# Biased attention heads: a band of near distances and four residue classes in place of the full square

## The reference

```python
DIL_PATTERNS = ((128, 1), (512, 4), (2048, 16))

def dilated_window_attention(q, k, v, rel_bias, window, dilation):
    w = window // (2 * dilation)
    ...
    mask = (np.abs(rel) <= w)[None] & ((key_l >= 0) & (key_l < L))[:, None, :]
    bias = jnp.transpose(rel_bias[t5_bucket(rel * dilation)], (2, 0, 1))
    logits = jnp.einsum('brnqhd,brnkhd->brnhqk', qs, kw) * (dh ** -0.5) + bias
    ...
    e = jnp.exp(logits - m)
    den = jnp.sum(e, axis=-1, keepdims=True)
    o = jnp.einsum('brnhqk,brnkhd->brnqhd', (e / den), vw)
```

## Time and profile before

| | us |
|---|---|
| median of 3 runs | 3556.62 (3554.47 to 3556.8) |
| profiled execution | 3552.48 |
| its span | 3550.7 |
| PE busy | 3451.8 (97%) |
| DVE busy | 2068.9 (58%) |
| ACT busy | 1715.8 (48%) |
| POOL busy | 1659.0 (47%) |

### The profile page before, as it was taken

One profiled execution on the slowest core, in us unless ns is written; L12 is line 12 of the kernel. 1 busy time (PEld: TensorE's weight loads), 2 busy tenths in 40 slices (PEclk: granted clock), 3 DMA queues, 4 the chain that ended last, 5 costly groups with the idle time before them and its releaser, 6 DMA issues. The chain is left out here.

```text
span 3550.7 us, 47741 instructions
## 1 busy us (share of the span) xinstructions
PE 3451.8 (97%) x17305; PEld 2858.6 (81%) x17305; DVE 2068.9 (58%) x3148; ACT 1715.8 (48%) x2973; POOL 1659.0 (47%) x1239
## 2 busy tenths in 40 slices
PE   8999999999899999999999999999998999999998
PEld 7788777778788888888777887777787888888886
DVE  4234888964745555455651358799366455554555
ACT  4343888974444434411353358789553344343113
POOL 1133554443477676423342435534345776763223
PEclk9999999999999999999999999999999999999999
DMA  5442320122122121422324413211232121213213
GB/s 181 128 104 75 77 75 23 42 84 96 53 68 78 58 78 58 144 80 82 118 70 135 127 52 90 57 34 32 75 107 67 62 78 59 78 58 137 95 66 119
DMA packets 247439, 292.81 MB, mean 82 GB/s; under 512 B 43244, under 2 KB 197182, under 8 KB 247167
## 3 DMA queue, kind: packets, MB, share of 16 engines
q1 hardware_dynamic: 247207, 289.76, 27.0%
HBM read 202.70 MB, written 80.31 MB: 80 GB/s over the span
## 5 line engine op out<-in xcount | busy, mean ns | idle before, releaser
L1709 DVE TENSOR_TENSOR pl<-ps,ph 128x512 fp32r<-128x512 f32 (+1 forms) x576 | 376.4, 654 | 66.4 <-ACT ps L1540 65.9
L1432 PE MATMUL ps<-q,k 97*128 97x512 f32 (+4 forms) x1296 | 387.1, 390 | 17.2 <-DVE pl L1709 7.0
L3098 DVE TENSOR_TENSOR y<-ps,y 128x512 f32<-128x512 f32 (+1 forms) x432 | 260.2, 602 | 230.8 <-PE ps L291 227.7
L1539 ACT ACTIVATE ph<-ps 128x512 fp32r<-128x512 f32 (+1 forms) x576 | 329.2, 572 | 135.2 <-PE ps L1432 130.6
L1540 ACT ACTIVATE ps<-ps 128x512 f32<-128x512 f32 (+1 forms) x576 | 328.4, 570 | 0.0
L1432 PEld LDWEIGHTS ps<-q,k 97*128 97x128 f32 (+2 forms) x1296 | 234.4, 189 | 86.3 <-DVE pl L1709 24.5
L1670 DVE TENSOR_REDUCE mx<-ps 128x1 f32<-128x512 f32 x352 | 242.0, 688 | 40.6 <-PE ps L1461 32.5
L1444 PE MATMUL ps<-ph,vh 128*128 128x512 f32 (+1 forms) x576 | 227.4, 395 | 0.0
L1445 PE MATMUL ps<-ph,vl 128*66 128x512 f32 (+1 forms) x576 | 219.7, 381 | 0.0
L1447 PE MATMUL ps<-pl,vh 128*128 128x512 f32 (+1 forms) x576 | 219.7, 381 | 0.0
L289 PE MATMUL ps<-hh,wh 128*128 128x512 f32 (+1 forms) x528 | 200.5, 380 | 10.1 <-PEq L283 6.2
(11 more groups left out here) (396 smaller groups left out, 10193.9 us busy)
## 6 DMA issues: line engine op xcount, KB each, us to landing
activations<-c_gate SPq DMA_DIRECT2D x44, 640.0 KB, 3.8
act_in<-activations SPq DMA_DIRECT2D x20, 1280.0 KB, 5.7
raw<-in_w_up SPq DMA_DIRECT2D x48, 512.0 KB, 4.9
up_raw<-in_w_up SPq DMA_DIRECT2D x40, 512.0 KB, 4.7
raw<-in_w_down SPq DMA_DIRECT2D x40, 512.0 KB, 3.5
heads<-stage SPq DMA_DIRECT2D x28, 640.0 KB, 3.5
rq<-heads SPq DMA_DIRECT2D x56, 320.0 KB, 4.0
raw<-in_w_in SPq DMA_DIRECT2D x32, 512.0 KB, 4.4
```

The costliest lines, as they stand in the source:

```text
L1432: mm = pe.matmul(out, a, b, start=(k == 0), stop=(k == len(prods) - 1))
L1539: act.activation(c.ph[g % RING][:, 0:w], scores, ACT.Exp, scale=STEP_SCALE[kind(h)]).then_inc(exp_done, 1)
L1709: dve.tensor_tensor(c.pl[g % RING][:, 0:w], bank(c, ST + g % 3, w), c.ph[g % RING][:, 0:w].bitcast(F32), ALU.subtract).then_inc(p_low, 1)
L3098: dve.tensor_tensor(y, bank(c, down_bank(it, u), w), y, ALU.add).then_inc(down_added, 1)
```

## The change

A biased head has ten steps in place of 18: two for the short sequence as before, four for the residue classes and four for the near band. In a class step all 256 keys of one residue modulo 4 meet the 256 queries of that residue, in two tiles of 128 keys; the table holds there only the distances above 64. In a near step two tiles of 128 keys meet the queries within 64 tokens of them, as four runs, one for each residue. Together they cover each unmasked pair once.

The q operand of the long sequence is stored by residue (`by_class`). The values are loaded a second time, by residue (`vh_class`, `vl_class`), and split by DVE. The tables `th` and `tl` are 1024 wide and come from new lines in memory (`distance_parts`). For the maxima of biased heads an fp32 table (`dense`) is loaded; PE fills two banks with 1024 scores of a tile of queries (`side_scores`) and DVE compares them in one instruction (`take_side`). The rest of the side work is placed by a table `side_at`.

```diff
-    STEPS = []
+    def class_step(r):
+        tiles, values = [], []
+        for u, half in enumerate((1, 0)):
+            tiles.append((slice(512 * half + r, 512 * half + 512, 4), 256 * r, CLASSES + P * u, 256 * u, 256, 0))
+            for q in range(2):
+                values.append(("class", 4 * half + r, 2 * q, P * r, 256 * u + P * q, P, 0, u == 0 and r == 0))
+        return tiles, values, {0: [0], 2: [2]}.get(r, []), []
+    def near_step(kts, ends):
+        for kt in kts:
+            qa, qb = max(0, kt * P - REACH), min(1024, kt * P + P + REACH)
...
+    SPLIT_STEPS += [class_step(r) for r in range(4)]
+    SPLIT_STEPS += [near_step((0, 7), []), near_step((1, 2), []), near_step((3, 4), [0]), near_step((5, 6), [2])]
...
+        elif kind(h) == "B":
+            for u, i in enumerate((2, 3, 4, 5, 6, 6, 7, 8, 9)):
+                put(h - 1, i, "side", h, u)
+            put(h - 1, 7, "row", h, 0)
+            put(h - 1, 8, "row", h, 1)
+            put(h, 0, "row", h, 2)
...
+                def side_scores(h, u):
+                    for n in range(2):
...
+                        mm = pe.matmul(bank(c, SIDE + n, w), c.q1[h % 3][:, q * P:q * P + P], c.k1[kv(h)][:, keys][:, ::-1], start=True, stop=True)
...
+                        region = c.ps[:, (SIDE + n) * 512:(SIDE + n) * 512 + w]
+                        dve.tensor_tensor_reduce(out=region, in0=region, in1=c.dense[h % 2][:, x0:x0 + w], scale=-1.0, scalar=3.0e38,
+                                                 op0=ALU.add, op1=ALU.min, accum_out=c.m[:, m0:m0 + 1]).then_inc(max_taken, 1)
...
+                def split_class_values(h):
+                    dve.tensor_copy(hi, raw).then_inc(class_hi, 1)
...
+                load_q(2)
+                for h in range(HEADS - 2):
+                    if kind(h) == "B":
+                        move_row(h, 2)
+                    if kind(h + 1) == "B":
+                        load_parts(h + 1)
+                    if kind(h + 2) == "B" and kind(h) == "B":
+                        load_dense(h + 2)
...
+                        for r in range(2):
+                            move_row(h + 1, r)
+                        load_q(h + 3)
...
+                sp.dma_start(c.s_parts, c.d_masked).then_inc(line_stored, 16)
+                sp.wait_ge(line_stored, 32)
...
+                    sp.dma_start(c.s_parts[:, CLASS_LINE + n0:CLASS_LINE + n1],
+                                 c.s_line[:, 3 + 4 * n0:3 + 4 * n1:4], allow_slow_non_contiguous=True).then_inc(line_stored, 16)
```

More of the change, by code:

```diff
@@ L1272, in row_tiles, with steps, place, step_width @@
         return ROW_TILES[r][1] - ROW_TILES[r][0]
+    def steps(h):
+        return SPLIT_STEPS if kind(h) == "B" else PLAIN_STEPS
+    FROM = [0]
+    for h in range(HEADS):
+        FROM.append(FROM[-1] + len(steps(h)))
+    G_TOTAL = FROM[HEADS]
+    G_END = G_TOTAL + PV_LAG + 4
+    PLACE = [(h, i) for h in range(HEADS) for i in range(len(steps(h)))]
+    def place(g):
+        return PLACE[g] if g < G_TOTAL else (HEADS, g - G_TOTAL)
+    def step_width(h, i):
+        return sum(tile[4] for tile in steps(h)[i][0])
@@ L1274, in third_row @@
+    OUTPUTS = [(h, block, g) for g, (h, i) in enumerate(PLACE) for block in steps(h)[i][3]]
+    OUTPUT = {(h, block): o for o, (h, block, _) in enumerate(OUTPUTS)}
     def third_row(h):
         return 19 - max_lead(h)
-    def side_work(h, i):
[L1280 to L1289, removed]
@@ new lines, in free_blocks @@
+    def free_blocks(h, i):
+        return [0, 2] if kind(h) == "B" and i == 2 else [] if kind(h) == "B" and i > 2 else steps(h)[i][2]
+    def side_work(h, i):
+        work = side_at.get((h, i), [])
+        return sorted(work, key=lambda item: (item[0] == "row", item[1], item[2]))
+    side_order = [item for g in range(G_TOTAL) for item in side_work(*place(g))]
+    side_banks, taken_after, turn = {}, {}, 0
+    TAKEN, READY = [0, NM], [0, 2]
+    for h in range(1, HEADS):
+        TAKEN.append(TAKEN[h] + (10 if kind(h) == "B" else NM))
+        READY.append(READY[h] + (0 if kind(h) == "B" else 2))
@@ L1401, in scores @@
                 def scores(g):
-                    h, i = divmod(g, NS)
-                    block, q0, w, kt, first, last = STEPS[i]
-                    out = bank(c, ST + g % 3, w)
+                    h, i = place(g)
+                    tiles, _, starts, _ = steps(h)[i]
                     q1, q2, k1, k2 = c.q1[h % 3], c.q2[h % 3], c.k1[kv(h)], c.k2[kv(h)]
@@ L1428, in scores @@
[L1428 to L1432 removed]
+                            pe.wait_ge(table_lo, 3 * (h - 3))
+                    for block in starts:
+                        if h == 0:
+                            pe.wait_ge(row_copied, block + 1)
+                        else:
+                            pe.wait_ge(row_landed[block], 16 * h)
@@ L1433, in scores @@
                     mm.then_inc(scored, 1)
                 def values(g):
-                    h, i = divmod(g, NS)
-                    block, q0, w, kt, first, last = STEPS[i]
-                    if first and h >= 1:
-                        pe.wait_ge(scaled, 3 * (h - 1) + block + 1)
+                    h, i = place(g)
+                    _, parts, _, ends = steps(h)[i]
+                    if h >= 1:
+                        for block in free_blocks(h, i):
+                            pe.wait_ge(scaled, OUTPUT[h - 1, block] + 1)
```

442 lines of the change are left out of this document (308 added, 134 removed).

## The result

The changed kernel takes 3635.58 us (median of 4 runs, 3624.27 to 3641.47), the kernel before in the same session 3555.55 us (3552.15 to 3556.8). The ratio is 1.0225, 95% interval 1.0207 to 1.0242: slower by 2.2%, where 1.8% faster was forecast.

What follows compares the result with a forecast made beforehand. The prediction took the biased stage as bound by TensorE, 95% of a head. Savings of 64 us in both layers, less 1 us in the first phase, off the 3556.62 us median gave 3494 us, range 3465 to 3558.

Steps and rivals of the forecast that it cites:

- The first phase, "I take 1 us": Before attention, the new line copies delay the residual's stores by 4 to 9 us; 0 to 4 on the path, 1 taken.
- -64 forecast: Attention in both layers: shorter biased stages, net of changes in heads 3 and 8, save 31.8 us a layer, 64 in both.
- The prediction's own sign of being wrong: End of the first phase: if it came after 76 us, the forecast would be wrong.
- "The longer of each counts", 97.8 us a stage: Biased heads 4 to 7: each step costs the longer of DVE's and PE's work; 97.8 us a stage against 130.8.
- the 0.108 taken as their floor: Biased heads' narrow matmuls: none can undercut its weight load, 108 ns for 128 columns.
- the rival of the fp32 price: Biased heads: narrow matmuls cost as much as plain fp32, PE 31.0 us a head, 3547 us in all; chance 0.28.
- the rival of the slow comparison: Biased heads' maxima: a 1024-wide DVE compare takes three times 1.14 us, 3632 us in all; chance 0.07.
- TensorE's sum, 20.6 us a head: PE's work in a biased head: score, value and maxima matmuls, narrow ones at their weight-load floor, total 20.6 us.
- The late third row, 1.15 us a head: Start of heads 5 to 7: PE waits for the third row of maxima, turned in step 0; 1.15 us a head.
- Head 3, "1.4 us": Head 3, ahead of the biased stage: it takes all of head 4's maxima, six more of 512 columns, 1.4 us.
- VectorE's sum: DVE's work in a biased head: compares, low parts, scaling and splits, 19.3 us next to PE's 20.6.
- the top of the fp32 case: Upper end of the own range, 3532 to 3565 us, if narrow matmuls cost as much as fp32; case chance 0.28.

Runs made afterwards that it cites:

- e14: Kernel with the splits on ScalarE, but GpSimd's query splits and DVE's output scaling touch neighbours instead of steps of four; 3532.73 us, 0.9945 of the kernel before the change.

## Why the prediction was wrong, step by step

- **The first phase, "I take 1 us"**: it is 34 us by the beginning of attention, 36 in all when measured alone. This is the step that failed most clearly, and 33 of the 140 us between the forecast and the result; the other 110 are the attention phases, -64 forecast and +46 measured. The range was made of two landings and the issues; the 1,912 numbers were counted but given no price, although what stands behind them in the queue is 5 MB that the phase's end waits for. The prediction's own sign of being wrong, a first phase that ends after 76 us, came true at 103.5.
- **"The longer of each counts", 97.8 us a stage**: 140.2 and 138.9. The widths, counts and prices of narrow matmuls held: four of 128 columns in 0.40 us at full clock, 0.10 each and so a little under the 0.108 taken as their floor, and the rival of the fp32 price is out. So did the comparison: 1.24 us, 1.15 from start to start, against 1.14; the rival of the slow comparison is out too. The waits between were missed. The turned rows 0 and 1 need a side bank and stand behind the side scores of their own step, so PE waits for the whole comparison, six times 1.4 us. The two units of step 6 wait in turn (3.03 us), behind a value split of 1.62 and 1.50 us, where the earlier trace rows have means of 0.57 and 1.03. Timeline of DVE there, with a wide comparison and its accumulator read:

```profile
537.40 1.62 DVE L691 CAST vh<-vt 128x640 fp32r<-128x640 f32 x1
539.05 1.50 DVE L693 TENSOR_TENSOR vl<-vt,vh 128x640 fp32r<-128x640 f32 x1
...
542.27 1.23 DVE L1902 CUSTOM_DVE_ANT_0 ps<-ps,dense 128x1024 f32<-128x1024 f32 x1 [0.94 <-PE ps L1646]
543.42 0.14 DVE L1902 DVE_READ_ACCUMULATOR2_ANT m<- 128x1 f32 x1
```

The cast of that split took 0.49, 1.62, 1.24 and 0.46 us in the four places of this stage. GpSimd was at work beside all four, and where the cast was short, GpSimd's own cast beside it was long (at 611.14 us 1.08 for 0.61). It looks as if the two engines hold each other up there; no run tried that alone. And the class values wait for the last head's output (5.6 us). The model took the longer of two sums a step, as if an engine could run ahead by a step; with one pair of banks and the waits in this order it can't. The sum left PE 15 us of waits a stage (97.8 less four times 20.6); it has 25. That is only 10 of the 42 us by which the first stage misses its sum; the rest is PE's busy time, 115.4 us for 82.4, and the next two points are about it.
- **TensorE's clock**: in no term of the sum. As the earlier trace rows show, it was at 0.9 or more of full throughout and at 1.00 in the stages, beside a PE that hardly waited; in the new stages, with 25 us of waits in each, it was 0.79 and 0.80. At 0.97 and 0.98 of full clock, in the run with the splits on ScalarE, the same matmuls are busy for 97.1 and 95.5 us instead of 115.4 and 114.5: 18 and 19 us of the stages. That is more than any wait by itself.
- **TensorE's sum, 20.6 us a head**: 23.9 busy at that clock. 16 strided loads of 0.12 us more are 1.9 of the difference; the others aren't resolved (a record's tail ahead of each wait counts as busy).
- **The late third row, 1.15 us a head**: not there. PE never waits for its transfer in either stage; its turn waits 0.38 us once, in the second.
- **Head 3, "1.4 us"**: 6 and 13 us (8 and 10 in the run with the lines packed). The wide comparisons stand beside head 3's full steps; with half of the comparison the part falls to 118.7 and 118.8 us.
- **VectorE's sum** held in size (19.3 a head, 20.4 measured), with the scaling at 1.02 us for 0.68, since it reads and writes in steps of four.

The chances put 12% on slower, by a slow comparison or the top of the fp32 case. None of the rivals had a mechanism in which PE's own waits make its work dearer.

With the repairs together (lines packed, rows first, units spread, the third row later, outputs scaled sooner, splits on ScalarE) the change pays, but less than computed: 3536.22 us, 0.56% under the kernel before where 1.8% was forecast, with stages of 108.7 and 107.1 us where the sum had 97.8. Its second stage:

```profile
2191.50:2298.60 107.10, 95.53 (x678) 87.42 (x677) 76.68 (x133) 70.14 (x150) 67.23 (x72) 0.98 0.34 82
```

What is still open: head 3's part costs 122 to 125 us in that kernel against 114 to 116 before, and which of its waits does that was not tried by itself.

## What to carry to other kernels

When a change takes work off the engine that bounds a kernel, forecast the waits first and the work second: list, for each buffer that two engines share, what the next user waits for, and ask whether the bounding engine would still be busy. If TensorE is not, its clock can fall, as here, where four matmuls of 128 columns then took 0.89 us instead of 0.40. The repair is to take the waits away. Products put exactly where TensorE waits show in one run how much of the loss is the clock; put ahead of work that others wait for, they brought nothing. And never let a DMA pick single numbers ahead of transfers that a phase's end waits for: a few instructions that pack them in SBUF cost nothing beside 31 us.

## What the runs showed that was not expected

- A DMA of single 4-byte numbers in DRAM: 1,912 of them, 7.6 KB, delay what stands behind them by some 31 us.
- A weight load with its columns in steps of four: 0.12 us more on TensorE than one of neighbours.
- Steps of four cost GpSimd 1.12 instead of 0.61 us for a cast of 512 elements (0.77 with the strides taken out, in e14) and 1.53 to 1.62 instead of 1.27 for a subtraction, and DVE 1.02 instead of 0.68 for a product from PSUM.
- PE's clock at 1.2 GHz behind waits of 1.4 to 3.0 us that follow each other, 0.79 and 0.80 of full clock over the stages; and at 0.96 and 0.91, with PE's own work the same, once fillers stood in three of the waits.
